# Hybrid decoder layer on one Trainium2 core: input sums made by transfers that add, one weight sum moved up, MLP weight loads moved back

## The reference, cut to what matters

```python
h = modulate(rms_norm(x), shift1, scale1)
proj = h @ w_in                      # 1024 x 1024 times 1024 x 3600
gq, gk, gv, g_lr, g_gate, hq, hf, hi, h_gate = jnp.split(proj, IN_OFFSETS, axis=-1)
# two groups of four heads: gated linear attention, and HGRN2 recurrence
o_gla = chunk_gated_linear_attention(...)    # chunks of 64 tokens
o_hgrn = chunk_gated_linear_attention(...)
x = x + gate1 * (concat([norm(o_gla) * silu(g_gate), norm(o_hgrn) * silu(h_gate)]) @ w_out)
h = modulate(rms_norm(x), shift2, scale2)
x = x + gate2 * (jnp.square(jax.nn.relu(h @ w_mlp1)) @ w_mlp2)
return rms_norm(x, final_norm_g)
```

## Time and profile before

| | |
|---|---|
| median of 3 runs | 1165.91 us (1165.58 to 1169.56) |
| profiled execution | 1166.44 us |
| its span, first to last instruction | 1164.7 us |
| TensorE busy | 1137.4 us, 98% |
| VectorE busy | 876.3 us, 75% |
| ScalarE busy | 612.9 us, 53% |
| GpSimd busy | 499.4 us, 43% |
| mean granted TensorE clock | 0.993 of full speed |
| moved by DMA | 180.44 MB, 155 GB/s on average |

### The profile page before, as it was taken

One profiled execution on the slowest core, in us unless ns is written; L12 is line 12 of the kernel. 1 busy time (PEld: TensorE's weight loads), 2 busy tenths in 40 slices (PEclk: granted clock), 3 DMA queues, 4 the chain that ended last, 5 costly groups with the idle time before them and its releaser, 6 DMA issues.

```text
span 1164.7 us, 15675 instructions
## 1 busy us (share of the span) xinstructions
PE 1137.4 (98%) x5555; PEld 939.3 (81%) x5555; DVE 876.3 (75%) x1048; ACT 612.9 (53%) x933; POOL 499.4 (43%) x318
## 2 busy tenths in 40 slices
PE   7999999899999999999999999999999999999996
PEld 6788788787878787888888888888888888788885
DVE  6898888877777677477976765677795884966776
ACT  7763564756566566345654555455664433424424
POOL 1021111534243344427534353344466675666741
PEclk9999999999999999999999999999999999999999
DMA  9777353044353549421455344544624637447203
GB/s 359 259 235 271 128 175 97 1 127 129 93 177 98 154 123 295 143 93 73 137 170 181 136 155 135 181 144 157 194 64 159 223 91 264 147 132 279 72 1 145
DMA packets 160549, 180.44 MB, mean 155 GB/s; under 512 B 7508, under 2 KB 119256, under 8 KB 157784
## 3 DMA queue, kind: packets, MB, share of 16 engines
q1 hardware_dynamic: 160472, 179.44, 46.4%
HBM read 138.51 MB, written 40.89 MB: 154 GB/s over the span
## 4 chain that ended last, share of the span: by engine, by line
PE 89%; DVE 4%; DMA 2%; ACT 2%; issue 1%; SPq 1%; POOL 1%; DVEq 0%; ACTq 0%
PE unit_bank L1742 16%; PE unit_bank L2156 9%; PE unit_bank L2158 9%; PE unit_bank L2157 9%; PE small_bank L2156 9%; PE small_bank L2158 9%; PE small_bank L2157 9%; PE unit_bank L2003 3%; PE small_bank L1742 3%; PE unit_bank L2005 3%; PE unit_bank L2004 3%; PE small_bank L1879 2%; DVE ada_acc L2257 1%; PE small_bank L1781 1%; DMA ada_slot<-in_w_ada_dram 1%
## 5 line engine op out<-in xcount | busy, mean ns | idle before, releaser
L997 POOL TENSOR_TENSOR wr_lo<-quarter,wr_hi 128x512 fp32r<-128x512 f32 x122 | 197.6, 1632 | 174.4 <-ACT wr_hi L1530 174.3
L2156 PE MATMUL unit_bank<-op_hi,wr_hi 128*128 128x512 f32 x452 | 176.5, 390 | 1.1 <-issue 1.1
L2158 PE MATMUL unit_bank<-op_hi,wr_lo 128*128 128x512 f32 x452 | 175.9, 389 | 0.0
L2157 PE MATMUL unit_bank<-op_lo,wr_hi 128*128 128x512 f32 x452 | 175.9, 389 | 0.0
L2156 PE MATMUL small_bank<-op_hi,wr_hi 128*128 128x512 f32 x448 | 174.5, 390 | 0.0
L2158 PE MATMUL small_bank<-op_hi,wr_lo 128*128 128x512 f32 x448 | 174.3, 389 | 0.0
L2157 PE MATMUL small_bank<-op_lo,wr_hi 128*128 128x512 f32 x448 | 174.3, 389 | 0.0
L1530 ACT ACTIVATE wr_hi<-wr_full 128x512 fp32r<-128x512 f32 x90 | 56.8, 631 | 173.3 <-DVE wr_full L2903 173.3
L2903 DVE TENSOR_TENSOR wr_full<-quarter,quarter 128x512 f32<-128x512 f32 x90 | 88.9, 989 | 56.3 <-PE small_bank L2158 23.0
L1530 ACT ACTIVATE wr_hi<-quarter 128x512 fp32r<-128x512 f32 x136 | 83.0, 626 | 90.5 <-PE unit_bank L2158 48.4
L1742 PE MATMUL unit_bank<-a_hi,w_hi 128*128 128x512 f32 x304 | 121.2, 399 | 0.8 <-DVE w_lo L2401 0.8
(11 more groups left out here) (366 smaller groups left out, 2397.2 us busy)
## 6 DMA issues: line engine op xcount, KB each, us to landing
quarter<-in_w_mlp_dram SPq DMA_DIRECT2D x128, 256.0 KB, 4.1
hidden_scratch<-hid SPq DMA_DIRECT2D x98, 256.0 KB, 2.4
ada_slot<-in_w_ada_dram SPq DMA_DIRECT2D x48, 512.0 KB, 6.1
op_full<-hidden_scratch SPq DMA_DIRECT2D x21, 1024.0 KB, 4.8
pair_quarter<-in_w_in_dram SPq DMA_DIRECT2D x32, 256.0 KB, 3.7
piece_x<-t_scratch SPq DMA_DIRECT2D x16, 512.0 KB, 4.1
piece_y<-t_scratch SPq DMA_DIRECT2D x32, 256.0 KB, 3.3
raw<-in_w_out_dram SPq DMA_DIRECT2D x16, 512.0 KB, 4.5
```

The costliest lines, as they stand in the source:

```text
L997: pool.tensor_tensor(wr_lo[slot][:, :, :], split_source(n), wr_hi[slot][:, :, :].bitcast(F32), ALU.subtract).then_inc(wr_lo_pool, 1)
L2156: pe.matmul(dst, wh, ah, start=opens, stop=False, skip_group_check=True)
L2157: pe.matmul(dst, wh, al, start=False, stop=False, skip_group_check=True)
L2158: mm = pe.matmul(dst, wl, ah, start=False, stop=k == KH - 1, skip_group_check=True)
```

## The change

Four things change.

1. The input sums are no longer made by VectorE. GpSimd issues transfers from SBUF to SBUF: `carry_over` copies a 1 MB block, `add_part` adds one into its destination (`accum_op=ALU.add`). There are four copies and nine additions. They stand in GpSimd's queue between the low parts of units 7 to 12, and each waits for what it depends on with two semaphores, `first_sum` and `other_sum`. Only additions are used, so the sums have other signs than before; to make up for it, S1, S2, S3 and S4 and two of the joins use turned signs, and S2 becomes one multiply-and-subtract instruction.
2. In group H0, S2 of pair 0 is made ahead of `decay` and `q_cum` instead of behind them.
3. In the output projection the four transfers that bring x back are spread: the two for the first token half go around the third weight tile's load, the two for the second half behind those of tiles 5 and 6. The first MLP quarters go behind tile 7 instead of tile 3.
4. Semaphores: the gain's load and the last `y_sum` counts use other semaphores, to make room for the two new ones. The places of `t4_hi` and `t4_lo` are swapped.

```diff
-        xs = [at(f"x_sum{i}", 8 * i, [P, KH, HALF]) for i in range(4)]
+        xs = {i: at(f"x_sum{i}", 8 * i, [P, KH, HALF]) for i in range(1, 4)}
...
-                    sp.wait_ge(t_made, T_MADE_0 + 4)
+                    sp.wait_ge(t_made, T_MADE_0 + 1)
...
-            for i in range(2):
-                load_x_back(i)
-            for v in range(2, 4):
+            load_x_back(0, 0)
+            load_out(2)
+            load_x_back(1, 0)
+            for v in range(3, OUT_HALVES):
                 load_out(v)
-            sp.wait_ge(normed, before("ss", 7))
-            sp.wait_ge(seventh_done, SEVENTH_0 + 4 * PAIRS)
-            for i in range(4):
-                for pr in range(2):
-                    load_quarter(0, pr, i)
-            for v in range(4, OUT_HALVES):
-                load_out(v)
+                if v in (5, 6):
+                    load_x_back(v - 5, 1)
+                if v == 7:
+                    sp.wait_ge(normed, before("ss", 7))
+                    sp.wait_ge(seventh_done, SEVENTH_0 + 4 * PAIRS)
+                    for i in range(4):
+                        for pr in range(2):
+                            load_quarter(0, pr, i)
...
+            def carry_over(dst, src, done):
+                pool.dma_start(dst[:, :, :], src).then_inc(done, 16)
+
+            def add_part(dst, part, k, half, done):
+                pool.dma_start(dst[:, :, :], blocks(part, k, half).bitcast(F32), accum_op=ALU.add).then_inc(done, 16)
+
+            def third_sum_begun():
+                pool.wait_ge(x_out, X_OUT_0 + 16 * KT)
+                pool.wait_ge(split_hi, 16)
+                pool.wait_ge(lo_dve, 16)
+                carry_over(xs[3], blocks(a_hi, 0, 1).bitcast(F32), first_sum)
+                pool.wait_ge(first_sum, 16)
+                add_part(xs[3], a_lo, 0, 1, first_sum)
+                pool.wait_ge(first_sum, 32)
+                carry_over(xs[1], xs[3][:, :, :], other_sum)
+
+            def two_sums(part, n):
+                pool.wait_ge(other_sum, 16 * n)
+                pool.wait_ge(first_sum, 16 * (n + 1))
+                add_part(xs[3], part, 1, 1, first_sum)
+                add_part(xs[1], part, 0, 0, other_sum)
+
+            def second_sum_begun():
+                pool.wait_ge(t3_stored, T3_STORED_0 + 32)
+                pool.wait_ge(other_sum, 48)
+                carry_over(xs[2], xs[1][:, :, :], other_sum)
+                pool.wait_ge(other_sum, 64)
+                add_part(xs[2], a_hi, 1, 1, other_sum)
+                pool.wait_ge(other_sum, 80)
+                add_part(xs[2], a_lo, 1, 1, other_sum)
+
+            def fourth_sum_part(part, n):
+                pool.wait_ge(first_sum, 16 * n)
+                add_part(xs[3], part, 1, 0, first_sum)
+
             for u in range(2, U_OUT):
                 low(u, u % 2)
+                if u == 7:
+                    third_sum_begun()
+                if u in (8, 9):
+                    two_sums((a_hi, a_lo)[u - 8], u - 7)
+                if u == 11:
+                    second_sum_begun()
+                if u == 12:
+                    pool.wait_ge(other_sum, 96)
+                    carry_over(xs[3], xs[2][:, :, :], first_sum)
+                    fourth_sum_part(a_hi, 5)
+            fourth_sum_part(a_lo, 6)
...
-                    act.wait_ge(t_made, T_MADE_0 + 7)
+                    act.wait_ge(other_sum, 48)
                     act.activation(t1_hi[:, :, :], xs[1][:, :, :], ACT.Copy).then_inc(t_high, 1)
                     act.wait_ge(unit_filled[1], 13)
-                    act.activation(blocks(a_hi, 0, 1), xs[3][:, :, :], ACT.Copy).then_inc(t_high, 1)
+                    act.wait_ge(other_sum, 96)
+                    act.activation(blocks(a_hi, 0, 1), xs[2][:, :, :], ACT.Copy).then_inc(t_high, 1)
...
-                        act.wait_ge(t_made, T_MADE_0 + 3)
+                        act.wait_ge(first_sum, 64)
                         act.activation(t3_hi[:, :, :], xs[3][:, :, :], ACT.Copy).then_inc(t_high, 1)
...
-                    act.wait_ge(t_made, T_MADE_0 + 9)
-                    act.activation(t4_hi[:, :, :], xs[2][:, :, :], ACT.Copy).then_inc(t_high, 1)
+                    act.wait_ge(first_sum, 112)
+                    act.activation(t4_hi[:, :, :], xs[3][:, :, :], ACT.Copy).then_inc(t_high, 1)
...
-                if name == "P1":
-                    dve.wait_ge(x_out, X_OUT_0 + 16 * KT)
-                    add_parts(xs[1], 0, 1, 0)
-                    add_parts(xs[0], 1, 1, 1)
-                if name == "H0":
-                    dve.wait_ge(t3_stored, T3_STORED_0 + 32)
-                    add_parts(xs[2], 0, 0, 4)
-                    subtract(xs[1], xs[1], xs[2], 5)
                 read_out(3)
-                if name == "H0":
-                    subtract(xs[3], xs[0], xs[1], 6)
...
-                    subtract(xs[3], xs[0], xs[1], 2)
...
                 read_out(6)
+                if own == "H":
+                    weight_sum_of(0, "S2")
...
-                if own == "H":
-                    weight_sum_of(0, "S2")
-                    add_parts(xs[2], 1, 0, 7)
-                    subtract(xs[2], xs[2], xs[3], 8)
...
-                    dst, a, b, op = pq[0], pq[3], pw_full[PAIR_PLACE[P7]], ALU.subtract
+                    dve.scalar_tensor_tensor(pq[0][:, :, :], pw_full[PAIR_PLACE[P7]][:, :, :], -1.0, pq[3][:, :, :],
+                                             ALU.mult, ALU.subtract).then_inc(pair_sum, 1)
...
-                    i, j, op = {"S1": (2, 3, ALU.add), "S3": (0, 2, ALU.subtract), "S4": (1, 0, ALU.subtract)}[kind]
+                    i, j, op = {"S1": (2, 3, ALU.subtract), "S3": (0, 2, ALU.subtract), "S4": (1, 0, ALU.add)}[kind]
...
-                dve.tensor_tensor(dst, a, b, ALU.add).then_inc(joined, 1)
+                dve.tensor_tensor(dst, a, b, ALU.subtract if c in ("22", "12") else ALU.add).then_inc(joined, 1)
```

More of the change, by code:

```diff
@@ L395, in hybrid_layer @@
         SB = [bank(f"small_bank{i}") for i in range(4)]
-        rows_loaded, gain_loaded = sem("rows_loaded"), sem("gain_loaded")
+        rows_loaded = sem("rows_loaded")
         x_loaded = [sem(f"x_loaded{i}") for i in range(8)]
@@ L445, in hybrid_layer @@
         acc_added = sem("acc_added")
-        y_sum = sem("y_sum")
+        first_sum, other_sum = sem("first_sum"), sem("other_sum")
         stored = sem("stored")
@@ L760, in load_mixed_back, with load_x_back @@
                 sp.dma_start(mixed[:, 0, :], mixed_dram).then_inc(mixed_back, 16)
-            def load_x_back(i):
+            def load_x_back(i, half):
                 sp.wait_ge(six_done, six_of(PAIRS - 1, P4 if i else P5))
-                for half in range(2):
-                    part = slice(half * HALF, (half + 1) * HALF)
-                    sp.dma_start(xT[:, 4 * i:4 * i + 4, part], x_dram[:, 4 * i:4 * i + 4, part]).then_inc(x_back[i][half], 16)
+                part = slice(half * HALF, (half + 1) * HALF)
+                sp.dma_start(xT[:, 4 * i:4 * i + 4, part], x_dram[:, 4 * i:4 * i + 4, part]).then_inc(x_back[i][half], 16)
             def load_out(v):
@@ L856, in _ @@
                     sp.dma_start(gain[:, :], final_g.rearrange("(a n) -> a n", a=1).broadcast_to([P, D])
-                                 ).then_inc(gain_loaded, 16)
+                                 ).then_inc(stored, 16)
                 if more and g:
@@ L921, in _ @@
                              out_stage[:, TT - 1, j * HALF:(j + 1) * HALF]).then_inc(stored, 16)
-            sp.wait_ge(stored, 16 * (TT + 1))
+            sp.wait_ge(stored, 16 * (TT + 2))
         @block.gpsimd
@@ L2402, in low_out @@
                                   ).then_inc(wlo_out, 1)
-            def add_parts(dst, k, half, n):
-                if n:
-                    dve.wait_ge(t_made, T_MADE_0 + n)
-                dve.tensor_tensor(dst[:, :, :], blocks(a_hi, k, half).bitcast(F32), blocks(a_lo, k, half).bitcast(F32), ALU.add
-                                  ).then_inc(t_made, 1)
-            def subtract(dst, a, b, n):
-                dve.wait_ge(t_made, T_MADE_0 + n)
-                dve.tensor_tensor(dst[:, :, :], a[:, :, :], b[:, :, :], ALU.subtract).then_inc(t_made, 1)
             def low_third():
@@ L2423, in low_second @@
                 dve.wait_ge(t_high, T_HIGH_0 + 3)
-                dve.tensor_tensor(blocks(a_lo, 0, 1), xs[3][:, :, :], blocks(a_hi, 0, 1).bitcast(F32), ALU.subtract
+                dve.tensor_tensor(blocks(a_lo, 0, 1), xs[2][:, :, :], blocks(a_hi, 0, 1).bitcast(F32), ALU.subtract
                                   ).then_inc(t_done, 1)
@@ L2429, in low_fourth @@
                 dve.wait_ge(t_high, T_HIGH_0 + 4)
-                dve.tensor_tensor(t4_lo[:, :, :], xs[2][:, :, :], t4_hi[:, :, :].bitcast(F32), ALU.subtract).then_inc(t_done, 1)
+                dve.tensor_tensor(t4_lo[:, :, :], xs[3][:, :, :], t4_hi[:, :, :].bitcast(F32), ALU.subtract).then_inc(t_done, 1)
             def group(name, gi, h):
@@ L2617, in weight_sum_of @@
```

(5 more changed lines are left out.)

8 lines of the change are left out of this document (4 added, 4 removed).

## The result

The changed kernel takes 1190.51 us (median of 4, 1188.51 to 1192.79); the kernel before, on the same chip, 1165.94. The ratio is 1.0204 with a 95% interval of [1.0172, 1.0236]. That is slower by 24.6 us, outside the predicted range of 1159 to 1183. The profiled execution took 1188.52 us with a span of 1186.8, against 1164.7 before. So 22.1 us of the span are to be explained; two of the four executions took 4 us more at a mean clock about 0.004 lower, which the trace does not cover.

What follows compares the result with a forecast made beforehand. TensorE, busy 98% of the span, was taken as the bound, so only its few waits and slow clock could be gained. Gains of 6.4 us (5.7 + 0.75) against 10.6 of cost gave +4.2: 1165.9 to 1170, range 1159 to 1183.

Steps and rivals of the forecast that it cites:

- The mechanism of the forecast's cost: Near 164: third sum 8.0 us late, TensorE waits 7.6 us for `vT`, then 3.0 us of slow clock; cost 10.6 us.
- The price of an add alone, 7.3 us: Adding transfers of 1 MB in both chains: 5.0 us of moving and 2.3 fixed.
- Two passes rather than one or three: Adds take 5.0 us of moving; rivals: copy's rate, 2.5 (in time, 0.33), or three passes, 7.5 (much slower, 0.17).
- The load order: Output projection: third weight tile lands about 6 us earlier, ending TensorE's wait for `w_lo`; gain 0.75 us.
- most of that can fall in the fixed times, and I add 2: First chain, 120 to 158: 12 us of weight and modulation loads on the same engines add only 2 us.
- my sum: First chain, step by step from near 120: copies and adds end at 161.6, with loads the third sum is whole at 163.6.
- the 3.0 that I took over: Slow clock expected behind TensorE's wait near 164: 3.0 us, the same as at the first pair before.
- the two adds of a pair to land together: First chain: two adds issued at once both land in 12.3 us.
- ends at 134.9 and is needed at 142.3: covered: Unit 8's low part on GpSimd, blocked by the first chain, still comes in time; no cost.
- price 0: Second chain: starts about 180, takes 31.5 us, GpSimd free at 211, low part of t1 in time; rival held GpSimd 0.08.
- so both waits and the slow clock behind them go: −5.7 us: First pair: TensorE's waits of 0.8 and 1.9 us for P7's and P2's low parts and 3.0 us of slow clock go.
- 2 us of cover: First pair: P7's and P2's low parts are done at 225.5 and 226.9; TensorE wants them at 227.9 and 228.9.

Runs made afterwards that it cites:

- Experiment 2: Changed kernel, but the last twelve loads of the modulation's weights bring 128 of 1024 columns: 1176.15 us, ratio 1.0088.
- experiment 5: Changed kernel with GpSimd's low part of t1 put ahead of the last adding transfer: 1187.03 us, ratio 1.0182.
- Experiments 6: S2 moved up alone in the kernel before: 1167.68 us, ratio 1.0021; S2 moved back behind `q_cum` in the changed kernel: 1188.70 us, ratio 1.0206.
- 8 to 11: Kernel before with new load order, S2 and a DVE sum earlier; then cumulatively `k_nat` and P6, P5's sum, partial sums earlier: 1166.75, 1167.30, 1167.28, 1167.27 us.
- experiment 7: Kernel before with only the load order at the output projection changed: 1165.17 us, ratio 0.9998.

## Why the prediction was wrong, point by point

**Right.** The mechanism of the forecast's cost: the third sum is late, ScalarE takes it in order, `vT` follows, TensorE waits at L1833 and runs slowly behind it. The price of an add alone, 7.3 us, nearly: the adds of the second chain are followed by the next issue after 7.9 and 8.0 us. Two passes rather than one or three: by the engines' time an add costs 6.0 us to a copy's 2.6, 2.3 times. The load order: its wait went, nothing came.

The Trainium skill (Collectives: The Full Stack, The bandwidth ceiling) has a reducing step at about half a copy's rate, for its two source reads. The trace agrees in kind, at 2.3 times.

**How the miss divides.** The forecast was +4.2 us and the span grew by 22.1, so 17.9 are missing. By the waits and the clock: 4.9 at the third sum (13.6 + 1.9 for 10.6), 2.9 at unit 8, 3.2 for the modulation, and 7.0 for `k_nat` and the slow clock around it, where the forecast had nothing left.

**Wrong, the first chain: "most of that can fall in the fixed times, and I add 2".** This term was mis-sized, and with unit 8 it is the largest part of the miss, 7.8 us. The rows had the engines busy with loads for 0.32 of the stretch. A chain in which each transfer waits for the one before has no gap to hide them in. Three of its five steps were longer than in my sum: 8.4 instead of 4.8, 11.2 instead of 7.3, 16.9 instead of 12.3 us; the second copy took its 4.9, and the last step 10.2 instead of 12.3. Together they took 51.6 us (121.1 to 172.7); my sum had 41.5 and the 2 for loads, from 120.1. Experiment 2 takes part of those loads away, and `t3_hi` starts 11.6 us earlier. So the forecast's 8 us became 17, and TensorE's 7.6 became 13.6. The slow clock behind it cost 1.9 us and not the 3.0 that I took over.

The sum also took the two adds of a pair to land together. They landed 7.9 and 15.8 us after their issue, and the third sum waited for the one that it does not need. A `two_sums` that waits for the third sum's add alone was not run. Its next add would then share the engines with the first sum's, so how much of the 9 us it would save is open.

**Wrong, "ends at 134.9 and is needed at 142.3: covered".** The same error, one step on: GpSimd was blocked until 141.3 by the transfers, the low part of unit 8 came at 143.6, and TensorE lost 1.5 us and 1.4 by the clock.

**Wrong, the second chain, "price 0".** I asked whether GpSimd would be in time for TensorE. The chain began at 194.7 and not at 180, and took 38.4 us to its last issue where my sum had 31.5 to the end, so GpSimd came to the low part of t1 at 233.8 and not before 211. And I did not ask whom its four subtractions would run beside. They met DVE's own at 233.6 and held it for 5.6 us; the wait for the modulation, 3.2 us, is that (experiment 5).

**Wrong, "so both waits and the slow clock behind them go: −5.7 us".** Both waits went (my 228.9 for P2's weights should have been 229.3, as below; it changes nothing). But I had looked for what else was due only on GpSimd and DVE, and took 2 us of cover for the end of it. ScalarE's `k_nat`, its copy of partial sums and the load of `piece_y` stood right behind. Experiments 6 and 8 to 11 took most of the waits for `pw_lo` away in five orders, and none gained; the 5.7 us did not come, and the place cost 1.3 more than it had (7.0). The 5.7 was itself the higher of two readings: in the trace of experiment 7, with the same waits, the place is 1.2 us shorter. That another operand stood behind was to be seen in the trace of before. There ScalarE makes `k_nat` at 235.07. TensorE's start on P2's weights, 231.98 less the waits of 1.87 and 0.81, is 229.3; twelve matmuls at 0.23 us apart bring it to `k_nat` at 232.1, three microseconds too soon.

**Left open.** The versions of experiments 6 and 8 to 11 are 1 to 2 us above the kernel before. The first pair is 0.5 to 1.7 us longer in their traces, but the spans of these profiled executions (1163.0 to 1166.2) are about its 1164.7, so that this is the whole reason is not shown. Not tried: which of the loads beside the chain delays it most, and an order that moves `k_nat` and the partial sums ahead without pushing the table loads back.

## What to carry to other kernels

Price a chain of dependent transfers at what it takes in the stretch where it runs, step by step, with the other queues' loads in the sum: here the loads that experiment 2 cut down had added 2.4 to 3.2 us to each of four steps, and they cannot be hidden in gaps that the chain does not have. Let a chain wait only for what it needs itself. Before a wait is counted as a gain, compute when TensorE would then reach each of its next operands, on every engine and queue, and compare with when the trace shows them made; a stall with other operands due right behind it is worth only the time until the next of them, and moving one ahead on a busy engine pushes the others back. And an engine that has been given work that blocks it is to be followed to the next instruction that it shares a resource with, not only to the next one that TensorE reads.

## What the runs showed of the hardware

- A 1 MB transfer within SBUF took 2.6 us of the sixteen engines as a copy and 6.0 us as an addition. From issue to landing an add took 7.6 to 8.3 us in the second chain (trace after), where other queues' packets took 12% of the engines' time; beside the modulation's weight loads 10.9, and in a pair 7.9 for one and 15.8 for the other.
- GpSimd was held about 1.28 us by the issue of most adds (1.77 at most), and 0.57 to 1.00 us by that of a copy.
- DVE's subtraction of 128 x 2048 elements took 7.91 us when it began 0.25 us before a row of four GpSimd subtractions of 128 x 512 (5.50 us), and 2.28 us alone; it ended 2.2 us after the row. A sum of 128 x 512 took 6.6 us instead of 0.68 when it began 0.56 us before such a row (experiments 2 and 6). Where GpSimd's row took 7.04 us instead (experiment 5), DVE lost 1.0 us in each of two instructions.
- The Trainium skill (SBUF — State Buffer, Who interferes with whom) says that a DVE instruction with two inputs in SBUF contends with a GpSimd instruction that reads SBUF; the rows of the point above agree.
- A wait of 13.6 us was followed by no more slow clock (1.9 us lost) than one of 4.6 us (2.4 us lost). Behind the same two short waits, 2.7 us together, 3.0 us were lost in one execution and some 1.2 less in another.
